# Scaling one head's attention probabilities on GpSimd instead of VectorE, in a two-layer transformer on one core

## What is computed

```
p = jax.nn.softmax(jnp.where(mask, logits.astype(jnp.float32), NEG_INF), axis=-1)
...
return jnp.einsum('bhqk,bkhd->bqhd', p.astype(v.dtype), v)
...
o = gi[..., 0:1] * o_cmp + gi[..., 1:2] * o_slc + gi[..., 2:3] * o_win
```

## Time and profile before

| what | value |
| --- | --- |
| median of 3 runs | 1412.97 us (1409.4 to 1413.98) |
| profiled execution | 1413.73 us, span 1412.0 us |
| TensorE busy | 1314.2 us, 93% |
| VectorE busy | 755.6 us, 54% |
| ScalarE busy | 648.9 us, 46% |
| GpSimd busy | 69.7 us, 5% |
| attention parts (units) | about 108 to 295 and 797 to 985 us |

### The profile page before, as it was taken

The page is one execution under the profiler, slowest core; times in us unless marked ns, Lnnn a source line. Parts: engine busy times, 40 slices in busy tenths (PEclk is TensorE's granted clock), DMA queues, the critical chain, the costliest instruction groups (busy, mean ns, idle before and its releaser), DMA issues.

```text
span 1412.0 us, 20009 instructions
## 1 busy us (share of the span) xinstructions
PE 1314.2 (93%) x6754; PEld 1067.9 (76%) x6754; DVE 755.6 (54%) x1200; ACT 648.9 (46%) x1171; POOL 69.7 (5%) x153
## 2 busy tenths in 40 slices
PE   5997888999999999999999978799999999999995
PEld 5995665678888888888889856566888888887884
DVE  6446567735555555533363656775455555564333
ACT  4335466634554544423352545576255445443232
POOL 1013001001000000000000401100000000000000
PEclk9998999999999999999999998999999999999998
DMA  6320100033333333332133110000333333333311
GB/s 205 114 84 1 61 1 1 16 105 80 104 97 89 90 108 100 105 100 94 51 101 95 53 59 2 1 16 16 104 105 89 90 108 99 89 92 117 95 54 59
DMA packets 121493, 107.69 MB, mean 76 GB/s; under 512 B 3875, under 2 KB 110981, under 8 KB 121425
## 3 DMA queue, kind: packets, MB, share of 16 engines
q1 hardware_dynamic: 119200, 102.71, 24.0%
q0 software_dynamic: 1360, 3.45, 0.9%
q10 hardware_dynamic: 864, 0.66, 0.1%
HBM read 104.71 MB, written 2.10 MB: 76 GB/s over the span
## 4 chain that ended last, share of the span: by engine, by line
PE 82%; DVE 8%; issue 5%; ACT 4%; DMA 1%; SPq 0%; DVEq 0%; ACTq 0%
PE ps L1306 24%; PE ps L1308 23%; PE ps L1307 23%; PE ps L1466 3%; PE ps L1501 3%; ACT probs L786 2%; DVE probs L1115 1%; DMA raw<-in_w_in_dram 1%; PE ps L1450 1%; DVE x L986 1%; ACT probs_t L796 1%; PE ps L1451 1%; DVE nmax L1097 1%; PE ps L1490 1%; DVE qf L1073 1%
## 5 line engine op out<-in xcount | busy, mean ns | idle before, releaser
L1306 PE MATMUL ps<-ht_hi,w_hi 128*128 128x512 f32 (+2 forms) x776 | 299.5, 386 | 20.4 <-DVE k_operand L1139 5.3
L1308 PE MATMUL ps<-ht_hi,w_lo 128*128 128x512 f32 (+2 forms) x776 | 298.1, 384 | 0.0
L1307 PE MATMUL ps<-ht_lo,w_hi 128*128 128x512 f32 (+2 forms) x776 | 297.8, 384 | 0.0
L534 DVE TENSOR_TENSOR w_lo<-raw,w_hi 128x1024 fp32r<-128x1024 f32 (+4 forms) x196 | 218.1, 1141 | 104.4 <-ACT w_hi L527 96.3
L527 ACT ACTIVATE w_hi<-raw 128x1024 fp32r<-128x1024 f32 (+4 forms) x196 | 186.5, 982 | 109.1 <-PE ps L1308 103.8
L1251 DVE SCALAR_TENSOR_TENSOR conv<-ps,cols,conv 128x510 f32<-128x510 f32 (+1 forms) x176 | 127.7, 746 | 179.9 <-ACT conv L890 173.8
L1306 PEld LDWEIGHTS ps<-ht_hi,w_hi 128*128 128x128 f32 x776 | 146.7, 189 | 48.9 <-issue 17.5
L1308 PEld LDWEIGHTS ps<-ht_hi,w_lo 128*128 128x128 f32 x776 | 146.8, 189 | 28.1
L1307 PEld LDWEIGHTS ps<-ht_lo,w_hi 128*128 128x128 f32 x776 | 146.7, 189 | 27.0
L1306 PE MATMUL ps<-w_hi,ht_hi 128*128 128x430 f32 (+1 forms) x392 | 147.8, 377 | 5.3 <-DVE ht_lo L973 4.7
L1308 PE MATMUL ps<-w_hi,ht_lo 128*128 128x430 f32 (+1 forms) x392 | 145.4, 371 | 0.0
(11 more groups left out here) (182 smaller groups left out, 1693.5 us busy)
## 6 DMA issues: line engine op xcount, KB each, us to landing
raw<-in_ffn_w_up_dram SPq DMA_DIRECT2D x88, 512.0 KB, 4.5
raw<-in_ffn_w_down_dram SPq DMA_DIRECT2D x44, 512.0 KB, 3.6
raw<-in_w_in_dram SPq DMA_DIRECT2D x32, 430.0 KB, 3.5
raw<-in_w_out_dram SPq DMA_DIRECT2D x16, 512.0 KB, 4.4
raw<-in_nsa_cmp_w_dram SPq DMA_DIRECT2D x8, 512.0 KB, 4.2
x<-in_x_dram SPq DMA_DIRECT2D x4, 512.0 KB, 6.4
out_dram<-probs SPq DMA_DIRECT2D x4, 512.0 KB, 2.6
raw<-in_mla_w_uq_dram SPq DMA_DIRECT2D x4, 384.0 KB, 3.4
```

The source lines that it names most:

```text
L534: last = nc.vector.tensor_tensor(d(w_lo)[:, :, d0:d1], r(raw)[:, :, r0:r1], d(w_hi)[:, :, d0:d1].bitcast(F32), ALU.subtract)
L1306: mm(o, lhs[0], rhs[0], start=start, stop=False)
L1307: mm(o, lhs[0], rhs[1], start=False, stop=False)
L1308: return mm(o, lhs[1], rhs[0], start=False, stop=stop)
```

## The change

From the fifth unit of each layer on (u >= 4) VectorE scales stream 0 only, and GpSimd scales stream 1. VectorE announces the scaling factors with a new semaphore `r_done`; GpSimd announces its half with `p_pool`, for which `turn` waits beside `p_done`. Since GpSimd's program now runs along the steps, its other work is sorted in between: the memsets come ahead of the GELU, each `twice` comes ahead of the scaling of its step, the passes over the compressed scores behind it.

```
+        def own_streams(u):
+            return (0, 1) if u < T else (0,)
...
+                def scale_second(u):
+                    n = (unit(u)[0] + 1) * P
+                    pool.wait_ge(r_done, at(r_done, l, u + 1))
+                    settle(pool)
+                    nc.gpsimd.tensor_scalar(probs[:, u % 3, 1, 0:n], probs[:, u % 3, 1, 0:n],
+                                            scaling(u)[:, u % 4, 1:2], None, ALU.mult).then_inc(p_pool, 1)
+                for s in range(1, U + 1):
...
+                    for g in range(G):
+                        if s == ITEM_STEP[ITEMS.index(("k", g))] + 1:
+                            pool.wait_ge(p_pool, at(p_pool, l, s - 1 - T))
+                            if g == 1:
+                                pool.wait_ge(pc_done, at(pc_done, l, 1))
+                            twice(g)
+                            pool.wait_ge(k_twice, at(k_twice, l, g + 1))
+                    if s - 1 >= T:
+                        scale_second(s - 1)
+                    if s == CS_MAX_STEP:
+                        pool.wait_ge(cs_max, at(cs_max, l, 1))
+                        tt(sc3, sc3, wide(0), ALU.subtract).then_inc(cs_sub, 1)
+                    if s == CS_SCALE_STEP:
+                        pool.wait_ge(cs_factor, at(cs_factor, l, 1))
+                        tt(sc3, sc3, wide(1), ALU.mult).then_inc(pc_done, 1)
...
-                    for s in range(2):
+                    dve.sem_inc(r_done, 1)
+                    for s in own_streams(u):
                         last = v.tensor_scalar(probs[:, u % 3, s, 0:n], probs[:, u % 3, s, 0:n],
                                                r[:, u % 4, s:s + 1], None, ALU.mult)
                     last.then_inc(p_done, 1)
...
                 def turn(u):
                     i = unit(u)[0]
                     pe.wait_ge(p_done, at(p_done, l, u + 1))
+                    if u >= T:
+                        pe.wait_ge(p_pool, at(p_pool, l, u - T + 1))
```

More of the change, by code:

```diff
@@ L126 @@
     "kl_done": H // 2,
-    "sc_done": U, "max_done": U, "exp_done": U, "p_done": U, "t_done": U, "pt_done": U, "pv_done": U // 2,
+    "sc_done": U, "max_done": U, "exp_done": U, "p_done": U, "p_pool": U - T, "r_done": U, "t_done": U, "pt_done": U, "pv_done": U // 2,
     "oh_done": H, "ol_done": H,
@@ L355, in hybrid_layers @@
         p_done = sem("p_done")
+        p_pool = sem("p_pool")
+        r_done = sem("r_done")
         t_done = sem("t_done")
@@ L562, in pair_done, with scaling @@
             return n * T // 2
+        def scaling(u):
+            return rgate if u >= U_MLA else rinv
+        def own_streams(u):
+            return (0, 1) if u < T else (0,)
         def score_banks(u):
@@ L632, in _ @@
                 last.then_inc(pos_ready, 1)
[L634 to L650, removed]
                 def twice(g):
@@ new lines, in _ @@
+                for s in range(1, U + 1):
+                    if s == HID_STEP + 1:
+                        pool.wait_ge(cmp_used, at(cmp_used, l, 4))
+                        settle(pool)
+                        for b in (kcz_hi, kcz_lo):
+                            last = nc.gpsimd.memset(b.bitcast(F32), 0.0)
+                        last.then_inc(kcz_ready, 1)
+                    if s == HIDT_STEP + 1:
+                        pool.wait_ge(hid_in, at(hid_in, l, 1))
+                        settle(pool)
+                        tt(gelu_t, hid_flat, hid_flat, ALU.mult).then_inc(pool_chain, 1)
+                        pool.wait_ge(pool_chain, ch.next())
+                        settle(pool)
+                        nc.gpsimd.tensor_scalar(gelu_t, gelu_t, 0.044715, 1.0, ALU.mult, ALU.add).then_inc(pool_chain, 1)
+                        pool.wait_ge(pool_chain, ch.next())
+                        tt(gelu_t, gelu_t, hid_flat, ALU.mult).then_inc(pool_chain, 1)
+                        pool.wait_ge(pool_chain, ch.next())
+                        settle(pool)
+                        nc.gpsimd.tensor_scalar(gelu_t, gelu_t, -50.0, None, ALU.max).then_inc(gelu_in, 1)
+                    for g in range(G):
[13 more added lines that the diff above has]
+                        tt(sc3, sc3, wide(1), ALU.mult).then_inc(pc_done, 1)
@@ L1105, in scale_probs @@
                     dve.wait_ge(dve_chain, ch.next())
-                    r = rinv
+                    r = scaling(u)
                     if u >= U_MLA:
@@ L1112, in scale_probs @@
                         dve.wait_ge(dve_chain, ch.next())
-                        r = rgate
-                    for s in range(2):
+                    dve.sem_inc(r_done, 1)
+                    for s in own_streams(u):
                         last = v.tensor_scalar(probs[:, u % 3, s, 0:n], probs[:, u % 3, s, 0:n],
```

## The result

The kernel after the change takes **1423.47 us** (median of 5 runs, 1421.17 to 1425.72), against 1413.07 for the kernel before, run beside it (1409.4 to 1414.21). The ratio is 1.0074, with a 95% interval of 1.0061 to 1.0087: 10.4 us slower, more than the 0.3% that can be told from no change. The forecast was 1411.8 us, no measurable change; the first rival, a slow GpSimd, had 1427.

The account below looks back on a forecast made before the run. TensorE, busy 93% of the span, was taken as the bound; -0.6 us a layer, -1.2 in two, took the profiled 1413.73 to 1412.5, and that execution stood 0.8 above the median: 1411.8 us, range 1406.5 to 1424.5.

Parts of the forecast that it names:

- the first rival: GpSimd's half becomes the wait, 1.61 us at 512 columns; 7.2 us a layer lost, 1427 us; chance 0.22.
- the fast end: GpSimd's scaling costs 0.84 ns a column and 0.18 us fixed, 0.61 us at 512 columns; slow end 1.61.
- The rest of the sum: Gains and losses at all places of a layer: -0.6 us, -1.2 in two layers.
- the extra queue instruction: TensorE's added wait, 44 a layer: 0.04 us showing at ten places, +0.4 us a layer; upper bound 2.6.
- the turn of unit 12: Turn behind the first casts: 0.4 us late, but VectorE's next item earlier; net -0.3 us a layer.
- unit 23's: Turn behind casts ending at 228.08: at 228.6 against 228.54, +0.1 us a layer.
- unit 24's wait of 0.69: Scaling starts 0.35 us earlier, complete 0.13 later than a pair would be: -0.2 us a layer out of this wait.
- the steady part: 512-column blocks without compressed values: row maximum 0.4 us forward, 0.1 gained four times, -0.4 us a layer.
- The order: The halves run one after the other, VectorE first: 1.05 us at 512 columns where the pair took 0.88.
- VectorE's busy time: Whole kernel: 88 scalings leave VectorE, so its busy time should be 30 to 35 us lower.
- Its point of decision, 0.72 us: GpSimd's time per scaling at which slack before the steady 512-column turn is gone.
- The rival of a gaining clock: TensorE's stretches behind unit 12 run at full clock in both layers: 4.5 us gained, 1407.3 us; chance 0.16.

Follow-up runs that it names:

- multiply-and-add run: Kernel after the change, with GpSimd's scaling as multiply by the factor, then add 0.0, instead of multiplication alone: 1412.82 us, 0.9999 of the kernel before.
- the later place: GpSimd's second casts put behind unit 24's scaling, the first behind unit 12's: 1405.15 and 1403.98 us in the kernel before, 1405.04 and 1405.34 with multiply-and-add split.
- Tensor by tensor: Kernel after the change, with GpSimd multiplying by the factor's column repeated along the row as a second tensor operand: 1416.41 us, 1.0024 of the kernel before.

## Why the prediction was wrong

- **The step that failed** is "I take the fast end, since the row of 289 ns holds a multiplication and does more arithmetic per element than the new instruction". More arithmetic was not more time. The row that had the new instruction's form, one operation and one input, was the maximum of 538 ns, and its 2.8 ns a column were near the truth of 2.47. Own time at 512 columns is 1.43 us, not 0.61. The Trainium skill (GPSIMD Engine Reference, section Elementwise) has one rate for bodies of one or two operations; the pair 1.43 and 0.56 us speaks against that here.
- **The rest of the sum held as a total, in part by luck.** With about the duration that it assumed, in the multiply-and-add run, the time was 0.9999 of the kernel before (0.9990 to 1.0008), where the sum had said -1.2 us. A 512-column scaling was complete 1.05 us after VectorE's start, as forecast, from 0.48 and 0.56 us instead of 0.44 and 0.61. The frame with the extra queue instruction cost 0.07% (-0.02 to 0.16%), where 0.8 us was given. But the places did not come out singly: the turn of unit 12 waited 1.75 us instead of 1.10 and unit 23's 2.46 instead of 1.99, both worse than forecast; unit 24's wait of 0.69 was gone, better than forecast. And a term was put at nothing without a reason: the steady part assumed that VectorE, once free, disturbs nothing, and at unit 32 its next instruction held GpSimd's half up and cost a wait of 0.89 us a layer.
- **The order.** "The order is VectorE, then GpSimd" held in the multiply-and-add run at every 512-column unit from 13 on in the first layer but one (244.26).
- **VectorE's busy time** fell by 27.6 us, not 30 to 35: the mean of a row counts an instruction of a pair in full, though back to back the second adds less (a pair of 512 columns takes 0.88 us, one alone 0.48), and some of VectorE's instructions were stretched beside the slow GpSimd (the 0.45 us above). The text had seen the first effect, and used the other number for the total.
- **Unit 12.** VectorE was released by the casts early and its item came forward, as forecast (183.12 for the item in the multiply-and-add run, against 182.9). But 0.28 us lay between the casts and the scaling, not 0.1, and the turn waited 1.75 us. Without the slow instruction this place still was no gain.
- **The rival** named the mechanism, and its sum was 3.5 us too high. It put the loss at four steady 512-column turns of 0.9; the trace has three there, of 0.55, 0.80 and 0.79, and 1.83 at 220.87, where 1.16 stood before the change. The 384-column turns behind unit 12, priced at 1.2 a layer, waited 5.5, 1.54 of it at unit 32. Its point of decision, 0.72 us, was read at one block (265.19) and was wrong as a rule: other turns, which waited for the scaling before the change already, have no slack at all, and cost followed duration over the whole range tried.
- **The clock.** The rival of a gaining clock gave 1407.3 us, taking 4.5 of the 5.6 us of work saved in two stretches. This change set little of it free: the clock behind unit 12 rose to 0.63 and 0.77, and TensorE's busy time fell by 0.9 us. Moving the casts gave 1.00 in both stretches and 1407.71 us. That this is so near the rival's price, which was for another change, is luck: low stretches went and came elsewhere too (0.72 from 198 to 204 us in that run).

## What to carry to other kernels

Price an instruction on GpSimd from a row of the same form (number of operations, inputs), not from one that seems to contain it; and where two rows disagree by a factor of two, take the range seriously or measure. VectorE and GpSimd did not share out this elementwise step: its halves came one behind the other, so such a move brings the result forward only if the second engine adds less than the part that it replaces. And look at what the engine that is freed does next: here its next instruction held the other half up. Before moving work off a stretched instruction, ask what stretches it: here the casts beside it were the cause, and a wait ahead of them (0.34%, and 0.5 to 0.7% with the later place) was worth more than the split, which gave nothing in its fast form.

## What the runs showed of the hardware

- **A GpSimd `tensor_scalar` with a lone multiplication was slower than with a second operation behind it**: 2.47 ns a column against 0.81, with fixed parts of about 0.16 us, as time added behind VectorE's half. Beside no scaling that started before them, 512 columns took 1.56 us (246.72, kernel after) and 0.70 us (244.26, multiply-and-add). Tensor by tensor lies between, at 1.64 ((0.92 - 0.29) / 384). A second operation does not always help: the maximum went from 538 to 650 ns with one.
- **Serial, but not for everything.** While GpSimd's 512-column scaling ran from 268.43, VectorE's 2-column multiplication of `rgate` at 269.55 took its usual 0.16 us and its row maximum 0.69; its 128-column scaling at 269.86 took 0.45 instead of 0.28 and ended just after GpSimd's. Beside GpSimd's wide two-input pass the same `rgate` instruction took 1.65 us. The Trainium skill (SBUF — State Buffer, section "SBUF: two separate sides") holds a VectorE instruction with two SBUF inputs back behind any GpSimd instruction that reads SBUF; the 1.65 us agree, the 0.16 don't.
- **VectorE can hold GpSimd up.** A GpSimd scaling of 384 columns took 1.82 us instead of 0.77 when VectorE's two-input instruction of 1.22 us started 0.23 us after it (251.27 and 251.50, multiply-and-add), and ended 0.37 us after VectorE's end.
- **A wait moved raised TensorE's clock** over some 7.5 us behind it, from 0.54 to 1.00, at nearly the same total idle time (97.8 us before, 99.0 with the casts behind in the kernel before), while a new stretch of 0.72 appeared from 198 to 204 us.
